# Two transformer blocks in fp32: the last layer norm with a split last bank, a root on ScalarE and a quarter scaled by GpSimd

## The chip, the cores and the metric

The kernel runs on one core of a Trainium2 chip. The metric is device time in microseconds (us), of one launch from start to end. The engines are TensorE (PE, matmuls; PEld is its weight loading), VectorE (DVE), ScalarE (ACT), GpSimd (POOL) and SyncE (SP, which issues the large transfers here). Each runs its own list of instructions in order, and they wait for one another by semaphores.

## The reference, cut to what matters

Two blocks follow each other on 256 tokens of 1024 features, all in fp32. The second block has two layers; each layer ends with a feed-forward part and a layer norm, and the last of these norms is what the change touches:

```python
ALPHA = (2.0 * DEPTH_2) ** 0.25

def layer_norm(x, g, b):
    mu = jnp.mean(x, axis=-1, keepdims=True)
    var = jnp.mean(jnp.square(x - mu), axis=-1, keepdims=True)
    return (x - mu) * lax.rsqrt(var + LN_EPS) * g + b

for l in range(DEPTH_2):                      # 2 layers
    ...                                       # feed-forward, norm, attention, norm
    x = layer_norm(ALPHA * x + 0.5 * swiglu(x, ffn2_w_in[l], ffn2_w_out[l]), ln_g[l, 2], ln_b[l, 2])
```

## The kernel before, in words

The 256 tokens are two tiles (t = 0, 1) of 128, one token to a partition, in `xres[:, t, :]` with 1024 columns. Weights come from HBM in units of 128x2048. Each unit is split by ACT into a high part (`whi`, line 519) and by DVE into the rest (`wlo`, line 527); a product of fp32 precision is three matmuls on them: `tile_mm`, lines 1561 to 1563, 512 columns wide. Line 1924 and line 1929 are the matmuls of the feed-forward's first half, the latter 256 columns wide.

The feed-forward's second half sums into four PSUM banks of 512 columns, bank 4 + 2t + h for token tile t and half h (`down_tile`). In the last step of it, `ffn_pe` goes through the token tiles one after the other: for tile 0 the four column blocks of the last but one unit, then half 0 and half 1 of the last unit, then the same for tile 1. Each half of the last unit is six matmuls, after which PE raises `y_done` (or `used` for the last one), and DVE may add that bank.

`norm_dve` then does, for each tile: two adds of a PSUM bank to `xres` with a sum over the columns (line 1302), the negative mean (line 1307), `cent = (xres + nmean) * ln_g` (line 1312) and, when the root is there, two scalings `xres = cent * lrs + ln_b` of 512 columns (line 1319). Tile 1's adds stand behind tile 0's scalings in DVE's list. `norm_act` (line 856) squares and sums 1024 columns on ACT as soon as the mean is there. `norm_pool` waits for that sum and makes 1 / sqrt(var + eps) on POOL in two instructions, a multiply-add (line 551) and a power of −0.5 (line 553), with a drain between them; the drain makes the first one's result readable for the second. SP waits for each scaling and stores its half tile to the output, four stores of 256 KB (line 485), and waits for all to land.

The function of an ACT instruction may need another table than the loaded one; a load then shows as ACT_TABLE_LOAD. `ffn_act` runs a dummy Silu on one column ahead of its first real one (line 882), so that the load happens there.

Order is set by hand: each engine's list is written out, nothing is planned by a cost model.

Of the kernel before, what the change touches and what calls it, by code (L numbers as in the profile page):

```python
# [8 lines left out]
P = 128  # L9
TOK = 256  # L10
TT = TOK // P
DM = 1024
KD = DM // P
# [9 lines left out]
LAYERS = 2  # L23
# [71 lines left out]
AHEAD = 6  # L95
ATT_ROPES = {0: (P_DQ, 0), 2: (P_DQ, 1), 4: (P_DK, 0), 6: (P_DK, 1)}
# [61 lines left out]
def build(nc, x, positions, ln1_g, w_in, q_norm_a, k_norm_a, q_norm_b, k_norm_b, sinks, w_branch_a,  # L158
# [19 lines left out]
    with ctx:  # L178
# [88 lines left out]
        nmean = little("nmean", [P, TT])  # L267
        mv = little("mv", [P, TT, 2])
# [91 lines left out]
        stored = sem("stored")  # L360
        up_tile = sem("up_tile")
# [78 lines left out]
        def _(sp):  # L440
# [40 lines left out]
            for t in range(TT):  # L481
                for h in range(2):
                    cols = slice(h * BW, (h + 1) * BW)
                    sp.wait_ge(xt_src, 4 * (XT1 + 4 * LAYERS) + 2 * t + h + 1)
                    sp.dma_start(out_r[:, t, cols], xres[:, t, cols]).then_inc(stored, 16)
            sp.wait_ge(stored, 32 * TT)
# [79 lines left out]
        def _(pool):  # L566
# [4 lines left out]
            pool.memset(half[:, :], -0.5)  # L571
            pool.memset(one_lam[:, :, :], 1.0)
# [35 lines left out]
            for l in range(LAYERS):  # L608
                q = 3 * l
                norm_pool(pool, q)  # L610

                for j in range(HALF):
                    pool.wait_ge(o_act, UNITS * l + HALF + j + 1)
                    rsqrt(pool, drs[:, j:j + 1], dss[:, j:j + 1], 1.0 / (2 * HD), EPS2, drs_ready)
                norm_pool(pool, q + 1)
                norm_pool(pool, q + 2)
# [241 lines left out]

        def hidden_act(act, g, u, ffn):

            w = FFN_H if ffn else BW
            for t in range(TT):
                act.wait_ge(used, u + 1)
                act.activation(hid_a[:, t, 0:w], ps[:, t, 0:w], ACT.Silu if ffn else ACT.Relu).then_inc(hid_act, 1)
# [38 lines left out]
        def _(act):  # L903
# [83 lines left out]
            for l in range(LAYERS):  # L987
# [49 lines left out]
                ffn_act(act, u + L_FFN2, g + FFN_S, 2 * l + 1, () if last else (u + L_UNITS, u + L_UNITS + 1))  # L1037
                for t in range(TT):
                    norm_act(act, 3 * l + 2, t)
                    if not last:  # L1040
                        xt_act(act, n + 4, toks=(t,))
# [249 lines left out]
        def norm_dve(dve, q, n, y, u, ffn, last=False):  # L1291
# [39 lines left out]
            if not last:  # L1331
                xt_dve(dve, n, toks=(0,), banks=banks, halves=(0,))
            centre(1)
            if not last:
                xt_dve(dve, n, toks=(0,), banks=banks, halves=(1,))
            scale(1)
            if not last:
                xt_dve(dve, n, toks=(1,), banks=banks)
# [48 lines left out]
        def _(dve):  # L1387
# [118 lines left out]
            for l in range(LAYERS):  # L1506
# [46 lines left out]
                norm_dve(dve, q + 2, n + 4, y + 5, u + L_UNITS - 1, True, last)  # L1553
# [407 lines left out]

        def ffn_pe(pe, u, g, f, n, late=None, banks=XT_BANKS):
# [11 lines left out]
            for t in range(TT):  # L1974
                for k in range(2):
                    for h in range(2):
                        m = down_tile(pe, before, k, h, t, False, False, k, 1 - par)
                if t == 0:
                    pe.wait_ge(lo_done, end + 1)
                    pe.wait_ge(ht_lo_done, 2 * (g + e) + 2)  # L1980
                else:
                    m.then_inc(used, 1)
                for h in range(2):
                    for k in range(2):
                        if t == h == k == 1 and late is not None:
                            late()
                        m = down_tile(pe, end, k, h, t, False, k == 1, k, par)
                    m.then_inc(used if t == h == 1 else y_done, 1)
# [172 lines left out]
```

## Time and profile before

| what | value |
| --- | --- |
| median of 3 runs | 1321.42 us |
| the three runs | 1321.1, 1321.42, 1323.9 us |
| span of the profiled execution, first to last instruction | 1321.2 us |
| PE busy | 1306.3 us, 99% of the span |
| PEld busy | 1102.8 us, 83% |
| DVE busy | 925.2 us, 70% |
| ACT busy | 640.9 us, 49% |
| POOL busy | 70.0 us, 5% |
| granted TensorE clock, mean | 0.997 of full speed |

The profile was taken in an execution of its own, of which it gives the span; the median of the runs is 0.2 us above it. Busy time is the time in which an engine ran an instruction that counts as work. Starts in the timeline are us from the span's start.

### The profile page before, as it was taken

The page shows a single profiled execution, that of the slowest core. Times are in us where ns is not written, and L with a number is a line of the kernel's source. Part 1 is how long each engine was busy: PE and PEld are TensorE (multiplying, and loading weights), DVE is VectorE, ACT ScalarE, POOL GpSimd, SP SyncE. Part 2 cuts the span into 40 slices and gives each one's busy share as a digit, 9 for nine tenths or more (in the row PEclk, how much of TensorE's full clock was granted, in tenths as well). Part 3 has the DMA queues.
Part 4 walks back from the last instruction along what each step waited for, and adds up shares of the span by engine and source line. Part 5 has one row for each costly group of instructions (what it writes and reads, how often), then busy time and mean ns, then how long its engine had stood idle before and what let it go on. Part 6 is the DMA issues. An engine that isn't in the chain of part 4 may idle for free.

```text
span 1321.2 us, 17217 instructions
## 1 busy us (share of the span) xinstructions
PE 1306.3 (99%) x6973; PEld 1102.8 (83%) x6973; DVE 925.2 (70%) x1188; ACT 640.9 (49%) x839; POOL 70.0 (5%) x145
## 2 busy tenths in 40 slices
PE   8999999999999999999999999999999999999997
PEld 7887788888888888887888888888888877888886
DVE  6698777766656666788876666776666888676665
ACT  6777635443335444457554444444443566544441
POOL 4121000000000000000300000000000003000000
PEclk9999999999999999999999999999999999999999
DMA  8543565555555555653565555465555444655550
GB/s 303 192 159 87 138 238 166 190 193 190 194 208 199 191 191 191 191 145 100 171 223 191 192 191 190 154 236 193 187 193 186 160 128 127 231 190 192 188 188 33
DMA packets 155167, 238.11 MB, mean 180 GB/s; under 512 B 4248, under 2 KB 110768, under 8 KB 155088
## 3 DMA queue, kind: packets, MB, share of 16 engines
q1 hardware_dynamic: 154704, 236.47, 54.7%
q8 instruction: 55, 0.90, 0.3%
q0 software_dynamic: 384, 0.54, 0.2%
q14 instruction: 24, 0.20, 0.0%
HBM read 235.95 MB, written 1.05 MB: 179 GB/s over the span
## 4 chain that ended last, share of the span: by engine, by line
issue 86%; PE 10%; POOL 2%; POOLq 1%; ACT 1%; DMA 0%; DVE 0%; SPq 0%; DVEq 0%; ACTq 0%
PE ps L1561 2%; PE ps L1563 2%; PE ps L1562 2%; POOLq L552 1%; POOL drs L553 1%; PE ps L1705 1%; PE ps L1628 1%; POOL lrs L553 1%; PE ps L1714 0%; DMA raw<-in_w_in_dram 0%; PE ps L1729 0%; ACT ebuf L734 0%; PE ps L1683 0%; PE ps L1603 0%; PE ps L1604 0%
## 5 line engine op out<-in xcount | busy, mean ns | idle before, releaser
L527 DVE TENSOR_TENSOR wlo<-raw,whi 128x2048 fp32r<-128x2048 f32 x172 | 391.8, 2287 | 129.2 <-ACT whi L519 129.2
L519 ACT ACTIVATE whi<-raw 128x2048 fp32r<-128x2048 f32 x197 | 369.8, 1905 | 22.3 <-DMA raw<-in_w_up_dram 11.1
L1924 PE MATMUL ps<-xt_both,whi 128*128 128x512 f32 x1504 | 358.7, 390 | 0.0
L1924 PEld LDWEIGHTS ps<-xt_both,whi 128*128 128x128 f32 x1504 | 279.1, 188 | 55.9
L1929 PEld LDWEIGHTS ps<-xt_both,wlo 128*128 128x128 f32 x1504 | 193.4, 191 | 7.6
L1241 DVE TENSOR_REDUCE hid_a<-ps 128x512 f32<-128x1024 f32 (+1 forms) x98 | 115.3, 1177 | 119.5 <-PE ps L1929 119.3
L1929 PE MATMUL ps<-xt_both,wlo 128*128 128x256 f32 x1504 | 195.7, 283 | 0.0
L1561 PE MATMUL ps<-whi,ht_hi 128*128 128x512 f32 x480 | 187.7, 391 | 0.0
L1562 PE MATMUL ps<-wlo,ht_hi 128*128 128x512 f32 x480 | 187.3, 390 | 0.0
L1563 PE MATMUL ps<-whi,ht_lo 128*128 128x512 f32 x480 | 186.8, 389 | 0.0
L877 ACT ACTIVATE hid_b<-hid_a 128x512 f32<-128x512 f32 x40 | 25.2, 631 | 236.5 <-DVE hid_a L1241 236.5
L1561 PE MATMUL ps<-whi,xt_both 128*128 128x512 f32 (+1 forms) x288 | 112.8, 392 | 0.0
L1562 PE MATMUL ps<-wlo,xt_both 128*128 128x512 f32 (+1 forms) x288 | 109.0, 378 | 0.0
L1563 PE MATMUL ps<-whi,xt_both 128*128 128x512 f32 (+1 forms) x288 | 109.0, 378 | 0.0
L1563 PEld LDWEIGHTS ps<-whi,ht_lo 128*128 128x128 f32 x480 | 90.1, 188 | 19.1
L1561 PEld LDWEIGHTS ps<-whi,ht_hi 128*128 128x128 f32 x480 | 90.3, 188 | 17.4
L1562 PEld LDWEIGHTS ps<-wlo,ht_hi 128*128 128x128 f32 x480 | 90.3, 188 | 16.8
L892 ACT ACTIVATE ht_hi<-hid_b 128x512 fp32r<-128x512 f32 x36 | 22.8, 633 | 94.1 <-DVE hid_b L1264 94.1
L500 DVE SCALAR_TENSOR_TENSOR wlo<-raw,g_cols,whi 128x512 fp32r<-128x512 f32 x80 | 56.1, 767 | 13.9 <-ACT whi L493 13.9
L1561 PEld LDWEIGHTS ps<-whi,xt_both 128*128 128x128 f32 x288 | 54.2, 188 | 12.0 <-issue 2.7
L1563 PEld LDWEIGHTS ps<-whi,xt_both 128*128 128x128 f32 x288 | 54.2, 188 | 10.4
L1562 PEld LDWEIGHTS ps<-wlo,xt_both 128*128 128x128 f32 x288 | 54.3, 189 | 8.6
(233 smaller groups left out, 1340.6 us busy)
## 6 DMA issues: line engine op xcount, KB each, us to landing
raw<-in_ffn_w_in_dram SPq DMA_DIRECT2D x80, 1024.0 KB
raw<-in_ffn_w_out_dram SPq DMA_DIRECT2D x44, 1024.0 KB
raw<-in_w_in_dram SPq DMA_DIRECT2D x36, 1024.0 KB
raw<-in_w_up_dram SPq DMA_DIRECT2D x16, 1024.0 KB
raw<-in_w_down_dram SPq DMA_DIRECT2D x16, 1024.0 KB
raw<-in_w_out_dram SPq DMA_DIRECT2D x8, 1024.0 KB
raw<-in_ffn_w_in_dram SPq DMA_DIRECT2D x16, 512.0 KB
raw<-in_w_out_dram SPq DMA_DIRECT2D x8, 512.0 KB
```

The costliest lines, as they stand in the source:

```text
L500: m = dve.scalar_tensor_tensor(wlo[j][:, cols], raw[j][:, cols], g_cols[:, k:k + 1], whi[j][:, cols].bitcast(F32), ALU.mult, ALU.subtract)
L519: act.activation(whi[j][:, :], raw[j][:, :], ACT.Copy).then_inc(hi_done, 1)
L527: dve.tensor_tensor(wlo[j][:, :], raw[j][:, :], whi[j][:, :].bitcast(F32), ALU.subtract).then_inc(lo_done, 1)
L553: pool.tensor_tensor(dst, dst, half[:, 0:dst.shape[-1]], ALU.pow).then_inc(done, 1)
L877: act.activation(hid_b[:, 0, :], hid_a[:, 0, :], ACT.Silu).then_inc(hid_act, 2)
L892: act.activation(ht_hi[s % 2][:, 0:2, :], hidden2, ACT.Copy).then_inc(ht_hi_done, 2)
L1241: return dve.tensor_reduce(hid_a[:, j, k * TOK:(k + n) * TOK].rearrange("p (k n) -> p k n", k=n), ps[:, b:b + n, :].rearrange("p k (j n) - ...
L1561: pe.matmul(o, hi[:, k, tok], block_of(whi, u, b, width), start=start, stop=False)
L1562: pe.matmul(o, hi[:, k, tok], block_of(wlo, u, b, width), start=False, stop=False)
L1563: return pe.matmul(o, lo[:, k, tok], block_of(whi, u, b, width), start=False, stop=stop)
L1924: pe.matmul(o(k).rearrange("p (j n) -> p j n", j=2), whi[w][:, block(b, k)], xt_both[:, :, b, :], start=b == 0, stop=False)
L1929: m = pe.matmul(o(k)[:, 0:TOK], wlo[w][:, block(b, k)], xt_hi[:, b, :], start=False, stop=b == KD - 1)
```

## The change

It touches the last norm of the second layer alone; the other norms stay as they are, and `norm_pool` is no longer called for the last one.

- The last bank of tile 1 is made in two halves by a new function, `last_columns`: first six matmuls of 256 columns into the first half of bank 7, then six into the first half of bank 0, which is free by then. The second half of bank 7 keeps the sum of the earlier units without the last one. DVE adds bank 6, the first half of bank 7, its second half, and then bank 0's 256 columns onto the same columns of `xres`. The sums of the pieces go to four columns of `quarter`, two of which are added in between.
- The mean is written twice, as `nmean` / 32 for ACT and as `nmean` for DVE. ACT squares `xres / 32 + nmean / 32`, so that its sum is the variance itself, drains, and takes the square root with the epsilon as bias; DVE takes the reciprocal of that and drains. A dummy root on one column stands in ACT's list behind the last feed-forward's copies.
- The scaling of tile 1 is cut: DVE does columns 0 to 511 and 512 to 767, POOL does 768 to 1023 in two instructions (a multiplication and an addition, with a drain between them).
- SP stores five pieces: two halves of tile 0, the first half of tile 1, POOL's quarter, DVE's last quarter, in this order.

```diff
+LAST_PIECES = ((0, slice(0, BW)), (0, slice(BW, DM)), (1, slice(0, BW)), (1, slice(DM - BW // 2, DM)),
+               (1, slice(BW, DM - BW // 2)))
+POOL_PIECE = 3
...
-            for t in range(TT):
-                for h in range(2):
-                    cols = slice(h * BW, (h + 1) * BW)
-                    sp.wait_ge(xt_src, 4 * (XT1 + 4 * LAYERS) + 2 * t + h + 1)
-                    sp.dma_start(out_r[:, t, cols], xres[:, t, cols]).then_inc(stored, 16)
-            sp.wait_ge(stored, 32 * TT)
+            for i, (t, cols) in enumerate(LAST_PIECES):
+                sp.wait_ge(pool_rows_out if i == POOL_PIECE else rows_out, 1 if i == POOL_PIECE else min(i + 1, len(LAST_PIECES) - 1))
+                sp.dma_start(out_r[:, t, cols], xres[:, t, cols]).then_inc(stored, 16)
+            sp.wait_ge(stored, 16 * len(LAST_PIECES))
...
+            pool.memset(eps2[:, :], EPS2 / ALPHA ** 2)
...
-                norm_pool(pool, q + 2)
+                if l < LAYERS - 1:
+                    norm_pool(pool, q + 2)
+            t, cols = LAST_PIECES[POOL_PIECE]
+            pool.wait_ge(last_factor, 1)
+            pool.tensor_scalar(cent[:, t, cols], cent[:, t, cols], lrs[:, t:t + 1], None, ALU.mult)
+            pool.drain()
+            pool.tensor_tensor(xres[:, t, cols], cent[:, t, cols], ln_b[:, cols], ALU.add).then_inc(pool_rows_out, 1)
...
+        def last_norm_act(act, q, t):
+
+            act.wait_ge(mean_ready, 2 * q + t + 1)
+            act.activation(squares[:, t, :], xres[:, t, :], ACT.Square, bias=nmean_root[:, t:t + 1], scale=1.0 / ROOT_DM,
+                           accum_out=mv[:, t, 1:2])
+            act.drain()
+            act.activation(lrs[:, t:t + 1], mv[:, t, 1:2], ACT.Sqrt, bias=eps2[:, 0:1]).then_inc(var_ready, 1)
...
+                if last:
+                    act.activation(scratch[:, :], ident[:, 0:1], ACT.Sqrt)
...
+        def last_norm_dve(dve, q, y, u):
...
+            def add(t, a, z, src, total, *ready):
+                xs = xres[:, t, a:z]
+                dve.wait_ge(*ready)
+                dve.scalar_tensor_tensor(xs, src, 0.5 / ALPHA, xs, ALU.mult, ALU.add, accum_out=total)
+
+            def mean(t, first, second):
+                dve.drain()
+                dve.tensor_scalar(nmean_root[:, t:t + 1], first, second, -1.0 / (DM * ROOT_DM),
+                                  ALU.add, ALU.mult).then_inc(mean_ready, 1)
+                dve.tensor_scalar(nmean[:, t:t + 1], first, second, -1.0 / DM, ALU.add, ALU.mult)
+                dve.drain()
...
+            def factor(t):
+                dve.wait_ge(var_ready, 2 * q + t + 1)
+                m = dve.reciprocal(lrs[:, t:t + 1], lrs[:, t:t + 1])
+                dve.drain()
+                return m
...
+            add(0, 0, BW, ps[:, 4, :], sums[:, 0, 0:1], y_done, y + 1)
+            add(0, BW, DM, ps[:, 5, :], sums[:, 0, 1:2], y_done, y + 2)
+            mean(0, sums[:, 0, 0:1], sums[:, 0, 1:2])
+            dve.wait_ge(g_loaded, 16 + 32 * (q + 1))
+            centre(0)
+            factor(0)
+            for t, cols in LAST_PIECES[:2]:
+                scale(t, cols)
+            add(1, 0, BW, ps[:, 6, :], quarter[:, 0:1], y_done, y + 3)
+            add(1, BW, DM - BW // 2, ps[:, 7, 0:BW // 2], quarter[:, 1:2], y_done, y + 4)
+            add(1, DM - BW // 2, DM, ps[:, 7, BW // 2:BW], quarter[:, 3:4], y_done, y + 4)
+            dve.drain()
+            dve.tensor_tensor(quarter[:, 2:3], quarter[:, 0:1], quarter[:, 1:2], ALU.add)
+            add(1, DM - BW // 2, DM, ps[:, 0, 0:BW // 2], quarter[:, 3:4], used, u + 1)
+            mean(1, quarter[:, 2:3], quarter[:, 3:4])
+            centre(1)
+            dve.drain()
+            factor(1).then_inc(last_factor, 1)
+            for i, (t, cols) in enumerate(LAST_PIECES[2:]):
+                if 2 + i != POOL_PIECE:
+                    scale(t, cols)
...
+        def last_columns(pe, u, par):
+
+            tok = slice(P, TOK)
+            for q, o in enumerate((ps[:, 7, 0:BW // 2], ps[:, 0, 0:BW // 2])):
+                for k in range(2):
+                    a = (2 * k + 1) * BW + q * BW // 2
+                    hi, lo = (w[SLOT_OF[u]][:, a:a + BW // 2] for w in (whi, wlo))
+                    pe.matmul(o, ht_hi[par][:, k, tok], hi, start=q == 1 and k == 0, stop=False)
+                    pe.matmul(o, ht_hi[par][:, k, tok], lo, start=False, stop=False)
+                    m = pe.matmul(o, ht_lo[par][:, k, tok], hi, start=False, stop=k == 1)
+                m.then_inc(y_done if q == 0 else used, 1)
```

## Rows read from the trace of the kernel before

**Rows 1.** The page: span, and busy time of PE and PEld.

```profile
span 1321.2 us, 17217 instructions
PE 1306.3 (99%) x6973; PEld 1102.8 (83%) x6973; DVE 925.2 (70%) x1188; ACT 640.9 (49%) x839; POOL 70.0 (5%) x145
```

**Rows 2.** Stretches: busy us (count) of PE, PEld, DVE, ACT, POOL, clock, DMA.

```profile
1314.00:1321.20 7.20, 0.00 (x1) 0.00 (x0) 3.72 (x8) 1.24 (x2) 0.74 (x2) 0.67 0.37 137
```

**Rows 3.** Timeline, tile 0's root and PE's last bank: start, duration, engine, line.

```profile
1309.63 1.15 ACT L856 ACTIVATE squares<-xres,nmean 128x1024 f32<-128x1024 f32 x1 [4.83 <-DVE nmean L1307]
...
1310.68 0.19 ACT L856 ACTIVATION_READ_ACCUMULATOR squares<-xres,nmean 128x1 f32 x1
...
1312.17 1.41 DVE L1319 SCALAR_TENSOR_TENSOR xres<-cent,lrs,ln_b 128x512 f32<-128x512 f32 x2 [1.20 <-POOL lrs L553]
...
1312.48 0.39 PE L1561 MATMUL ps<-whi,ht_hi 128*128 128x512 f32 x1
...
1313.61 0.39 PE L1563 MATMUL ps<-whi,ht_lo 128*128 128x512 f32 x1
```

**Rows 4.** Timeline, tile 1 from its adds to its scalings.

```profile
1313.51 0.68 DVE L1302 SCALAR_TENSOR_TENSOR xres<-ps,xres 128x512 f32<-128x512 f32 x1
...
1314.12 0.68 DVE L1302 SCALAR_TENSOR_TENSOR xres<-ps,xres 128x512 f32<-128x512 f32 x1
...
1314.89 0.21 DVE L1307 TENSOR_SCALAR nmean<-sums 128x1 f32<-128x1 f32 x1
...
1315.20 1.28 DVE L1312 SCALAR_TENSOR_TENSOR cent<-xres,nmean,ln_g 128x1024 f32<-128x1024 f32 x1
1316.19 0.19 ACT L856 ACTIVATION_READ_ACCUMULATOR squares<-xres,nmean 128x1 f32 x1
1316.46 0.19 POOL L551 TENSOR_SCALAR lrs<-mv 128x1 f32<-128x1 f32 x1 [4.32 <-ACT squares L856]
1316.80 0.54 POOL L553 TENSOR_TENSOR lrs<-lrs,half 128x1 f32<-128x1 f32 x1
1317.38 1.41 DVE L1319 SCALAR_TENSOR_TENSOR xres<-cent,lrs,ln_b 128x512 f32<-128x512 f32 x2 [0.89 <-POOL lrs L553]
```

**Rows 5.** Timeline of SP at the last store; DMA issues with us to landing.

```profile
1318.82 0.33 SPq L485 DMA_DIRECT2D out_dram<-xres  x1
...
out_dram<-xres SPq DMA_DIRECT2D x4, 256.0 KB, 2.0
```

**Rows 6.** Groups by form, whole span: busy us, mean ns, idle before.

```profile
L606 POOL TENSOR_SCALAR gates<-gates 128x1024 f32<-128x1024 f32 x4 | 5.0, 1240 | 44.0 <-ACT gates L686 44.0
L553 POOL TENSOR_TENSOR rstd<-rstd,half 128x10 f32<-128x10 f32 x2 | 4.5, 2254 | 0.3
...
L739 ACT ACTIVATE esink<-sink,ntop 128x1 f32<-128x1 f32 x16 | 3.8, 286 | 0.0
...
L1097 DVE TENSOR_TENSOR ob_lo<-ps,ob_hi 128x256 fp32r<-128x256 f32 x4 | 1.7, 420 | 1.5 <-ACT ob_hi L754 1.5
...
L1080 DVE RECIPROCAL rden<-den 128x1 f32<-128x1 f32 x8 | 1.2, 154 | 0.3 <-ACT ebuf L729 0.3
```

**Rows 7.** Timeline of PEld: eight weight loads for 256 columns, then the next.

```profile
1298.96 1.13 PEld L1929 LDWEIGHTS ps<-xt_both,wlo 128*128 128x128 f32 x8
...
1300.02 1.70 PEld L1924 LDWEIGHTS ps<-xt_both,whi 128*128 128x128 f32 x8
```

**Rows 8.** Timeline, DVE (first of a pair, then the pair) and POOL at once.

```profile
110.83 0.74 DVE L500 SCALAR_TENSOR_TENSOR wlo<-raw,g_cols,whi 128x512 fp32r<-128x512 f32 x1
110.83 2.20 DVE L500 SCALAR_TENSOR_TENSOR wlo<-raw,g_cols,whi 128x512 fp32r<-128x512 f32 x2
111.34 1.15 POOL L606 TENSOR_SCALAR gates<-gates 128x1024 f32<-128x1024 f32 x1 [7.60 <-ACT gates L686]
```

**Rows 9.** Groups by form, whole span: table loads at line 882, squares at 856.

```profile
L856 ACT ACTIVATE squares<-xres,nmean 128x1024 f32<-128x1024 f32 x12 | 13.8, 1153 | 29.8 <-DVE nmean L1307 29.8
...
L882 ACT ACT_TABLE_LOAD x3 | 3.8, 1283 | 0.1
```

More of the change, by code:

```diff
@@ L12 @@
 DM = 1024
+ROOT_DM = 32
+assert ROOT_DM ** 2 == DM
 KD = DM // P
@@ L267, in build @@
         nmean = little("nmean", [P, TT])
+        nmean_root = little("nmean_root", [P, TT])
+        quarter = little("quarter", [P, 4])
+        eps2 = little("eps2", [P, 1])
         mv = little("mv", [P, TT, 2])
@@ L360, in build @@
         stored = sem("stored")
+        rows_out = sem("rows_out")
+        last_factor = sem("last_factor")
+        pool_rows_out = sem("pool_rows_out")
         up_tile = sem("up_tile")
@@ L1037, in _ @@
                 ffn_act(act, u + L_FFN2, g + FFN_S, 2 * l + 1, () if last else (u + L_UNITS, u + L_UNITS + 1))
+                if last:
+                    act.activation(scratch[:, :], ident[:, 0:1], ACT.Sqrt)
                 for t in range(TT):
-                    norm_act(act, 3 * l + 2, t)
-                    if not last:
+                    if last:
+                        last_norm_act(act, 3 * l + 2, t)
+                    else:
+                        norm_act(act, 3 * l + 2, t)
                         xt_act(act, n + 4, toks=(t,))
@@ L1289, in ffn_dve, with norm_dve @@
                 split_lo_half(dve, v, 1)
-        def norm_dve(dve, q, n, y, u, ffn, last=False):
+        def norm_dve(dve, q, n, y, u, ffn):
             def add(t, h):
@@ L1330, in norm_dve @@
             mean(1)
-            if not last:
-                xt_dve(dve, n, toks=(0,), banks=banks, halves=(0,))
+            xt_dve(dve, n, toks=(0,), banks=banks, halves=(0,))
             centre(1)
-            if not last:
-                xt_dve(dve, n, toks=(0,), banks=banks, halves=(1,))
+            xt_dve(dve, n, toks=(0,), banks=banks, halves=(1,))
             scale(1)
-            if not last:
-                xt_dve(dve, n, toks=(1,), banks=banks)
+            xt_dve(dve, n, toks=(1,), banks=banks)
@@ new lines, in last_norm_dve, with centre, scale @@
+        def last_norm_dve(dve, q, y, u):
[9 more added lines that the diff above has]
+                dve.drain()
+            def centre(t):
+                dve.scalar_tensor_tensor(cent[:, t, :], xres[:, t, :], nmean[:, t:t + 1], ln_g[:, :], ALU.add, ALU.mult)
+            def factor(t):
[3 more added lines that the diff above has]
+                return m
+            def scale(t, cols):
+                dve.scalar_tensor_tensor(xres[:, t, cols], cent[:, t, cols], lrs[:, t:t + 1], ln_b[:, cols],
+                                         ALU.mult, ALU.add).then_inc(rows_out, 1)
+            add(0, 0, BW, ps[:, 4, :], sums[:, 0, 0:1], y_done, y + 1)
[19 more added lines that the diff above has]
+                    scale(t, cols)
@@ L1552, in _ @@
                 ffn_dve(dve, u + L_FFN2, g + FFN_S, () if last else (u + L_UNITS, u + L_UNITS + 1))
-                norm_dve(dve, q + 2, n + 4, y + 5, u + L_UNITS - 1, True, last)
+                if last:
+                    last_norm_dve(dve, q + 2, y + 5, u + L_UNITS - 1)
+                else:
+                    norm_dve(dve, q + 2, n + 4, y + 5, u + L_UNITS - 1, True)
         def block_of(w, u, b, width=BW):
@@ L1983, in ffn_pe @@
                 for h in range(2):
+                    if t == h == 1 and late is None:
+                        last_columns(pe, end, par)
+                        break
                     for k in range(2):
-                        if t == h == k == 1 and late is not None:
+                        if t == h == k == 1:
                             late()
```

## Prediction

> **What bounds the kernel now.** I read the page first: TensorE (PE) is busy for 99% of the span, so nearly all of the 1321.2 us belongs to matmuls, which this change leaves alone except for the last bank [rows 1]. Then the stretches: after 1314.0 PE has nothing to do, and the 7.2 us up to the end of the span hold 3.7 us of VectorE (DVE), 1.2 us of ScalarE (ACT) and 0.7 us of GpSimd (POOL) [rows 2]. This tail is a chain in which one engine waits for another, and it is all that the change can move, apart from what happens to its start. Last I read the timeline of the tail, instruction by instruction, because the chain of waits merges it too much.
>
> In the tail the reader is to see five links. (1) PE ends its last matmul at 1313.61 + 0.39 = 1314.00 [rows 3]. (2) DVE adds the last two banks of token tile 1, at 1313.51 and 1314.12; the second follows the first by 0.61 us and starts 0.12 after PE's end, so here DVE and PE end almost together. The mean follows at 1314.89, which is 0.77 after the start of the last add. (3) ACT's sum of squares ends at 1316.19 + 0.19 = 1316.38. (4) POOL computes the root in two instructions from 1316.46 on, and DVE starts to scale at 1317.38, so the root costs 1.00 us from ACT's end. (5) Two scalings take 1.41, to 1318.79 [rows 4]; SP issues the last of four stores 0.03 later, which takes 0.33 to issue and lands 2.0 after [rows 5]; the span ends 2.4 after the issue's start. For token tile 0 the same root takes 1.30 (1310.87 to 1312.17) [rows 3], and DVE goes straight from its scalings to the adds of tile 1 (1312.17 to 1313.51, 1.34 us): a quicker root there lets the adds of tile 1 start sooner.
>
> The profile's page gives a span of 1321.2; the three runs have a median of 1321.42, so 0.2 lies around the span. I sum changes against the span and add 0.2.
>
> **The change, part by part.** *The root on ACT.* It removes two POOL instructions per token tile, and adds a drain, a root of 128x1 on ACT, and a reciprocal and a drain on DVE. A root is not in the trace; the nearest row is another function of ACT on 128x1 with a bias column, 0.286 [rows 6]. I take that; from below, no cost at all would make the step 0.29 cheaper, and the dearest nearby bound is a whole squaring of 1024 columns, 1.15 [rows 3], which nothing in a 128x1 form suggests. The reciprocal is 0.154 [rows 6]. Between engines I take the 0.08 of the row from ACT to POOL (1316.38 to 1316.46) for each drain, and 0.04 from POOL's end (1316.80 + 0.54 = 1317.34) to DVE's start for a wait on DVE [rows 4]. From ACT's end to the scalings: 0.08 + 0.286 + 0.04 + 0.154 + 0.08 = 0.64 us, against 1.30 for tile 0 and 1.00 for tile 1. Saved: 0.66 and 0.36. The bounds of the sum are 0.35 and 1.5.
>
> The table for the root is loaded ahead: a load lasts 1.283 [rows 9] and stands after ACT's last copy, behind which ACT idles 4.83 us before the squaring [rows 3]. It costs nothing; without this cover it would cost its 1.28. The removed norm of POOL frees nothing else, since nothing is queued behind it. One more small memset at the start of POOL is hidden by its wait for the first weights.
>
> *A second nmean.* Each mean now writes two columns, the scaled one first, which releases ACT as before. The centring starts later by at most one small DVE instruction (0.15). It ended at 1315.20 + 1.28 = 1316.48 [rows 4], and becomes about 1316.70 (with the late start of the mean, below), while the root comes at 1316.82: hidden, by 0.1. If that cover were gone, at most 0.15.
>
> *The last bank on PE.* Six matmuls of 512 columns, 0.226 apart (1312.48 to 1313.61 in five steps) [rows 3], become twelve of 256. Weight loads of a 256-column group are (1300.02 − 1298.96) / 8 = 0.133 apart [rows 7]. Twelve take 1.59 against 1.36, so PE ends 0.22 later, 1314.22 (the last starts at 1312.48 + 11 x 0.133 = 1313.94 and takes 0.28). The first half of the bank is there at 1312.48 + 5 x 0.133 + 0.28 = 1313.43.
>
> *The adds of tile 1.* The scalings of tile 0 start at 1310.87 + 0.64 = 1311.51, so the first add starts 1.34 later, at 1312.85 (its bank is ready at 1312.48 − 0.23 + 0.39 = 1312.64). At +0.61, 1313.46, come two adds of 256 columns. A DVE instruction from PSUM of 256 columns takes 0.42 [rows 6] against 0.68, so each is 0.27 shorter: the second starts at 1313.80, and from there to the next small instruction it is 0.77 − 0.27 = 0.50: 1314.30. That one sums two columns, at most 0.15: 1314.45. By then PE is done (1314.22), so the split bank is not what DVE waits for. The last add and its drain take 0.50 again, and the mean starts at 1314.95, **0.06 later than before** (1314.89). Three small adds with one more sum eat up what tile 0 saved. Bounds: −0.1 with small instructions that overlap, +0.2 without. So the gain of the bank's split is nil: 0.66 earlier at the start, 0.06 later at the end.
>
> *The scalings.* Tile 1's can start at 1316.38 + 0.06 + 0.64 = 1317.08, 0.30 earlier. DVE now has 512 and 256 columns; the latter is 0.27 shorter than 0.74, 0.47, and alone it would end at 1317.08 + 0.67 + 0.47 = 1318.22. POOL has 256 columns in two instructions, a multiplication and an addition. The multiplication: 193 ns at 1 column [rows 4] and 1240 at 1024 [rows 6] make 1.02 ns a column, so 0.19 + 0.26 = 0.45. An addition of two tensors on POOL is not in the trace. Bounds: 0.45 if the second input is free; 0.54 (a power of 128x1 [rows 4]) + 256 x 2.05 = 1.07 if each input costs a pass. A power on POOL costs far more per column: 2.254 at 10 columns [rows 6] against 0.54 at one, 0.19 a column, which would make 49 us of 256. I leave that end out of the range with a small chance of its own, because the multiplication by the same engine shows that plain arithmetic costs 1.02 ns a column, and an addition is nearer to it. I take 0.7, between the other two. The GPSIMD Engine Reference of the Trainium skill (Elementwise, side-by-side cycle accounting) gives about 2.6 cycles per column for such an addition, 0.56 us at its 1.2 GHz before any overhead; my sum would be the same within 0.1 by it.
>
> Do POOL and DVE run side by side? The trace has this case. DVE's pair of 128x512 with both inputs in SBUF normally takes 1.41 [rows 4]. At 110.83 such a pair took 2.20; its first had the usual 0.74, and POOL's multiplication ran from 111.34 to 112.49. The second ended at 113.03, 0.54 after POOL [rows 8]: it stood still while POOL read, and ran afterwards. So the two take turns. The last scalings read cent and ln_b, both in SBUF, so this applies to them. If DVE is first: it lets go at 1317.08 + 0.67 = 1317.75; POOL multiplies to 1318.20; DVE's quarter ends 0.54 − 0.27 = 0.27 later, 1318.47; POOL adds to 1319.17. SP's queue holds the stores in the order half, POOL's quarter, DVE's last quarter, so the last store waits behind POOL's: issues at 1319.20 and 1319.53, against 1318.82 before, **+0.7**. If POOL is first (1317.08 to 1317.53), DVE's half ends 0.54 later at 1318.07, POOL adds to 1318.77, the issues stand at 1318.80 and 1319.13: **+0.3**. The last instructions before are a near tie (a wait on POOL against a drain on DVE, 0.08 each), so I take +0.5.
>
> *The stores.* One more issue (0.33) is in the sums. The last store has 128 KB instead of 256. Landing is 2.0 for 256 KB [rows 5]; smaller may be quicker by anything from 0 to half of it. I take 0.2.
>
> Sum: +0.5 − 0.2 = +0.3; 1321.2 + 0.3 + 0.2 around = **1321.7 us**. It is no change that can be measured: about 0.2% (2.6 us) is what a measurement of this kernel tells from none.
>
> **Rivals.**
> 1. *POOL and DVE do not hinder each other.* POOL: 1317.08 + 0.45 + 0.15 + 0.7 = 1318.38; issues at 1318.41 and 1318.74, so −0.1, and −0.3 with the smaller store: **1321.1**. For it: the multiplication is short and might fit into DVE's gaps. Against it: rows 8.
> 2. *A table switch comes onto the path (slower).* If the set with the root lacks the square, ACT must load before each root. The loads before the squares hide in ACT's idle time (4.83, and as much for tile 1); those before the two roots do not: tile 0's delays its scalings by 1.28 and with them the adds, tile 1's adds 1.28 again: 2 x 1.283 = 2.57, **1324.3**. It decides as slower once the two cost over 2.4. Against it: the square of this norm ran twelve times with no load at its line, while the loads at the line that prepares Silu stand elsewhere [rows 9]; it seems to be in every set that was in use. The Trainium skill, in ScalarE: Activation LUTs (What ACT_TABLE_LOAD costs), puts 1.38 us of drain on top of each switch; by that the rival would give 1327.0. No run here shows such a drain. The preload would take 2.7 of its 4.83 and still be hidden.
> 3. *The whole saving shows* (DVE's adds start without small gaps, POOL's add is 0.45, the store is twice as quick): 0.3 + 0.4 + 0.3 gives **1320.4**. A gain over 0.2% would need more than a third of the whole tail, and none of its parts is that large.
>
> **How the numbers follow.** Forecast (turns taken, 1321.4 to 1322.1) 0.60; rival 1 0.25; rival 3 0.06; rival 2 0.05; anything else, a POOL addition many times dearer above all, 0.04. The range 1320.4 to 1323.0 leaves out rival 2 and the last, and on its upper side holds what the three runs differ by. Faster by over 0.2% 0.02, within 0.2% 0.92, slower 0.06.
>
> **What would show it.** Right: the root and reciprocal put DVE's scalings of tile 0 at about 1311.5 and those of tile 1 near 1317.1; the mean of tile 1 stands near 1314.9; one of DVE's or POOL's last instructions is stretched well beyond 0.75 or 0.45; the last store is issued at 1319.1 to 1319.5, behind POOL's. Wrong: a table load between a square and a root; an addition on POOL above 1.1; a last issue before 1318.8; PE's end beyond 1314.5; or PE's stretches before 1307 not the same as now, which no part of the sum foresees.

## The result, and the profile after

The changed kernel is slower: 1325.56 us median (1325.0 to 1327.39, 5 runs) against 1321.42. The ratio to the kernel before is 1.0029, 95% interval 1.0018 to 1.0040. The forecast was 1321.7, no change that can be measured; the range ended at 1323.0. The profiled execution took 1326.12 with a span of 1324.0. The executions of the kernel before fall into two groups, at 1320.8 to 1322.6 and at 1322.9 to 1325.8 us, so a median of few can jump by 2 us, and the interval of the ratio is what counts.

The tail first. Rows of the timeline of the changed kernel, which answer to [rows 3, 4] (start, duration, engine, line):

```profile
1312.28 0.18 ACT L880 ACTIVATION_READ_ACCUMULATOR squares<-xres,nmean_root 128x1 f32 x1
...
1312.81 0.29 ACT L883 ACTIVATE lrs<-mv,eps 128x1 f32<-128x1 f32 x1 [0.34 <-issue]
...
1313.38 1.41 DVE L1392 SCALAR_TENSOR_TENSOR xres<-cent,lrs,ln_b 128x512 f32<-128x512 f32 x2
...
1314.71 0.68 DVE L1373 SCALAR_TENSOR_TENSOR xres<-ps,xres 128x512 f32<-128x512 f32 x1
...
1315.39 0.28 PE L2051 MATMUL ps<-whi,ht_lo 128*128 128x256 f32 x1
...
1316.75 0.21 DVE L1377 TENSOR_SCALAR nmean_root<-quarter 128x1 f32<-128x1 f32 x1
...
1318.06 0.19 ACT L880 ACTIVATION_READ_ACCUMULATOR squares<-xres,nmean_root 128x1 f32 x1
...
1318.90 1.29 DVE L1392 SCALAR_TENSOR_TENSOR xres<-cent,lrs,ln_b 128x512 f32<-128x512 f32 x2
1318.91 1.47 POOL L632 TENSOR_SCALAR cent<-cent,lrs 128x256 f32<-128x256 f32 x1 [183.49 <-DVE lrs L1387]
1320.53 0.72 POOL L634 TENSOR_TENSOR xres<-cent,ln_b 128x256 f32<-128x256 f32 x1
```

And SP's timeline at the last store of the changed kernel:

```profile
1321.65 0.43 SPq L496 DMA_DIRECT2D out_dram<-xres  x1
```

The same matmuls start 1.6 us later here than in the kernel before (matmul number 6951 at 1310.22 against 1308.63), so 1.6 has to be taken off. Then the scalings of tile 1 start at 1317.3, 0.1 earlier than before, but GpSimd's multiplication lasts 1.47, and its quarter is done at 1320.53 + 0.72 = 1321.25. The last store, behind it in SP's queue, is issued at 1321.65, which is 1320.05 in the time of before, 1.2 later. The tail, from a matmul that all kernels have (number 6951) to the end of the span, grew from 12.62 to 13.74 us: **1.1 us lost in the tail**.

A smaller part lies outside the span. The time exceeds the span by 1.74 to 1.87 us in every execution on record of a kernel with four stores, and by 2.07 to 2.24 in every one of a kernel with five: 0.3 us, in the changed kernel too. Whether the fifth store is the reason, or something else that those kernels share, was not tried.

That is not all. Two rows of the stretches of the kernel before, then of the changed kernel (us; busy us with count of PE, PEld, DVE, ACT, POOL; clock; DMA share; GB/s):

```profile
20.00:24.00 4.00, 4.00 (x18) 3.00 (x17) 4.00 (x7) 4.00 (x8) 2.95 (x26) 1.00 0.67 159
...
32.00:36.00 4.00, 4.00 (x19) 3.34 (x18) 3.87 (x6) 2.01 (x4) 2.01 (x3) 1.00 0.48 139
```

```profile
20.00:24.00 4.00, 4.00 (x18) 3.03 (x17) 4.00 (x7) 4.00 (x8) 2.16 (x22) 1.00 0.78 54
...
32.00:36.00 4.00, 1.53 (x7) 1.01 (x6) 4.00 (x7) 4.00 (x8) 4.00 (x8) 1.00 0.70 222
```

In the changed kernel TensorE stands still for 2.5 of the four microseconds from 32. From 20 to 24 the DMA engines are busier than before and move a third as much. The waits of the changed kernel in its first 45 us (who waited for whom, us in total, times, longest; "issue" is a wait for nothing that the profile shows) lead back:

```profile
POOL lrs L562 <- issue: 5.6, 1, 5.6
...
ACT proj L671 <- POOL lrs L564: 4.9, 1, 4.9
...
DVE pos_f L1421 <- DMA dlam<-in_diff_lambda_dram: 3.0, 1, 3.0
...
PE ps L1641 <- ACT proj L671: 2.5, 1, 2.5
```

TensorE waits for ACT's first projection reads, these for the norm on GpSimd, and GpSimd stands 5.6 us behind its constants' loads, until `dlam` has landed: the profile names no releaser there, but GpSimd goes on at 27.76, 0.5 after the landing (issued at 18.72, landed 8.5 later), and in the kernel with the dummy root below at 26.52, 0.6 after it (18.14 + 7.8). The rows of DMA issues say how long the loads took, first of the kernel before, then of the changed kernel (KB, us to landing):

```profile
dlam<-in_diff_lambda_dram POOLq DMA_DIRECT2D x1, 256.0 KB, 3.9
...
sink<-in_swa_sink_dram POOLq DMA_DIRECT2D x1, 8.0 KB, 4.0
```

```profile
dlam<-in_diff_lambda_dram POOLq DMA_DIRECT2D x1, 256.0 KB, 8.5
...
sink<-in_swa_sink_dram POOLq DMA_DIRECT2D x1, 8.0 KB, 6.5
```

The change touched none of these loads, and in the code near them only one memset; three new small tiles also move where they land by 96 bytes. Among the packets of GpSimd's queue, those of 256 and 512 bytes (16 each, the two `sink` loads) took 18 and 32 ns on average in the kernel before, and 878 and 1117 ns in the changed one. The 4 and 64 byte packets of the same queue took 12 and 25 ns in both, so it is these two loads that are slow and not small packets as such. **This loss at the start is the larger part**, and the experiments had to find its cause.

### The profile page after: what moved, and what is told of

Its sections match the earlier page's. It is cut to its first block, busy times and chain, and to the rows that moved or that the text cites. A ratio compares the mean times of both kernels' runs of the same rounds, so it can differ in the third digit from the quotient of the medians.

```text
span 1324.0 us, 17245 instructions
## 1 busy us (share of the span) xinstructions
PE 1305.9 (99%) x6979; PEld 1102.7 (83%) x6979; DVE 926.5 (70%) x1197; ACT 643.1 (49%) x843; POOL 69.8 (5%) x144
## 4 chain that ended last, share of the span: by engine, by line
issue 86%; PE 8%; POOL 2%; ACT 1%; POOLq 1%; DMA 1%; SPq 0%
PE ps L1641 2%; PE ps L1643 2%; PE ps L1642 2%; POOLq L563 1%; POOL drs L564 1%; PE ps L1785 1%; POOL lrs L564 1%; DMA raw<-in_w_in_dram 1%; ACT whi L504 0%; PE ps L1794 0%; PE ps L1809 0%; ACT ebuf L752 0%; PE ps L1763 0%; ACT proj L671 0%; POOL gain L590 0%
```

## The experiments

A table of what each run showed; the text on each follows. Tail: from matmul 6951 to the end of the span. Packets: mean ns of the 256 and 512 byte packets on GpSimd's queue. Stall: by how much TensorE's matmuls slip between number 131 and 141 (near 34 us) against the second profile of the kernel before. Half clock: whether the trace has a stretch of 3.4 us at half the granted clock near 10 us. In the two kernels that load the sinks late, the packets are those of 37 to 40 us.

```
kernel                   median    ratio (95%)               tail   packets     dlam  stall  half clock
before                   1321.42   -                         12.62    18   32   3.9   0.0    yes
before_again             1321.40   one run                   12.63    18   28   4.5   -      no
after                    1325.56   1.0029 (1.0018-1.0040)    13.74   878 1117   8.5   2.7    no
after_again              1325.72   one run                   13.74   905 1020   7.7   1.9    no
after_new_tiles_last     1325.42   1.0025 (1.0017-1.0034)    13.75   766 1096   7.3   1.5    no
before_padded_96         1322.25   0.9999 (0.9989-1.0008)    12.62    18   32   3.9   0.0    no
before_one_memset        1322.47   0.9998 (0.9989-1.0007)    12.55    18   27   4.9   0.0    no
after_memset_late        1325.28   1.0022 (1.0013-1.0030)    13.75  1193  901   5.8   0.0    yes
after_dve_scales_all     1324.64   1.0013 (1.0004-1.0022)    12.73  1003 1036   8.0   2.2    no
before_root_on_act       1323.04   1.0009 (1.0000-1.0017)    12.19   668 1428   8.0   2.1    no
before_dummy_sqrt        1323.72   1.0017 (1.0008-1.0026)    12.62   627 1143   7.8   1.9    no
before_dummy_exp         1324.25   one run                   12.62    18   47   3.9   0.0    yes
after_silu_for_sqrt      1322.94   1.0008 (1.0000-1.0017)    13.46    19   27   4.3   0.0    no
after_gpsimd_alone       1326.11   one run                   14.57  1153  893   6.0   0.0    yes
before_dummy_gelu        1323.91   1.0010 (1.0001-1.0019)    12.61   855 1097   7.5   1.6    no
before_sinks_late        1323.42   1.0004 (0.9995-1.0013)    12.61   109   30   5.3   0.0    no
root_on_act_sinks_late   1323.37   1.0001 (0.9992-1.0010)    12.21   158  686   4.8   0.0    yes
```

The medians of the kernel before in the four sets of runs were 1321.97, 1322.34, 1321.55 and 1321.26; a ratio is made within its set. Where the clock was halved, TensorE was already late by 1.6 to 3.0 us at number 131, and the late norm held it up no more. A stall of 0.0 in such a trace is no proof of a quick start; there the packets and `dlam` tell.

**Addresses.** The three new small tiles stand in the middle of the small ones and move `dlam`, `subg` and the sinks by 96 bytes. One kernel puts them last, one moves the tiles in the kernel before:

```diff
@@ after_new_tiles_last
-        nmean_root = little("nmean_root", [P, TT])
-        quarter = little("quarter", [P, 4])
-        eps2 = little("eps2", [P, 1])
...
         drs = little("drs", [P, TT * 4])
+        nmean_root = little("nmean_root", [P, TT])
+        quarter = little("quarter", [P, 4])
+        eps2 = little("eps2", [P, 1])
@@ before_padded_96
         nmean = little("nmean", [P, TT])
+        pads = [little(f"pad{j}", [P, 1]) for j in range(3)]
```

> The changed kernel, with its three new small tiles (nmean_root, quarter, eps2) allocated behind all the others, so that every older tile has the address it had before the change. Theory A (addresses): moving the small tiles by 96 bytes made the constants' loads from GpSimd's queue slow (dlam lands after 8.5 us instead of 3.9), which holds GpSimd's first norm and costs TensorE 2.7 us near 34 us of the span. Then this kernel has its dlam landing near 4 us, no stall of TensorE at 34 us, and only the tail's cost is left: 1.2 us over the kernel before, about 1322.6. Theory B (timing or chance: the constants' loads collided with the weights' loads in the profiled execution because TensorE's and ScalarE's start was earlier there): no difference to the changed kernel, 1325.5. Theory C (more instructions or semaphores at the start): 1325.5 as well.

> The kernel before, with three unused tiles of one column (96 bytes in all) allocated behind nmean, which moves the later small tiles by as much as the change does; nothing else differs and no instruction is added. Theory A (addresses): 2.7 to 2.9 us slower than before, about 1324.3, with dlam landing at 6 to 9 us and a stall of TensorE near 34 us. Theories B and C: the time of before, 1321.4.

> The kernel before, profiled once more. It shows whether the slow start belongs to an execution or to a kernel. Theory A: TensorE's matmul number 131 at the time of the first profile (33.8 us, or a little earlier without the stretch at half clock that the first profile had), dlam landing at 3.9 us. Theory B: a start like the changed kernel's may appear here too, with dlam at 8 us.

> The changed kernel, profiled once more. Theory A: dlam lands at 6 to 9 us again and TensorE stalls by about 2.7 us near 34 us again. Theory B: the landing may be at 4 us and the stall gone. The tail is as in its first profile in both: GpSimd's multiplication about 1.4 us long, the last store issued 17.2 us after the first matmul of the last but one unit.

Theory A was mine and falls twice: with the old addresses the start stays slow, with the moved ones it stays quick. B falls too: the slow packets came back in each profile of the changed kernel and in none of the kernel before. The second profile of before also mends a number of the prediction: its span is 1319.6 with a time of 1321.40. So 1.8 us lie around a span (2.1 in the changed kernel), and the first profile, with its halved clock, was of an execution 1.6 us slower than this one.

**The memset, and parts of the change.**

```diff
@@ before_one_memset
             pool.memset(half[:, :], -0.5)
+            pool.memset(spare[:, :], 1e-5)
@@ after_memset_late
             pool.memset(half[:, :], -0.5)
-            pool.memset(eps2[:, :], EPS2 / ALPHA ** 2)
...
+            pool.memset(eps2[:, :], EPS2 / ALPHA ** 2)
             pool.drain().then_inc(mask_pool, 1)
@@ after_dve_scales_all
-            pool.tensor_scalar(cent[:, t, cols], cent[:, t, cols], lrs[:, t:t + 1], None, ALU.mult)
-            pool.drain()
-            pool.tensor_tensor(xres[:, t, cols], cent[:, t, cols], ln_b[:, cols], ALU.add).then_inc(pool_rows_out, 1)
...
-                if 2 + i != POOL_PIECE:
-                    scale(t, cols)
+                scale(t, cols)
@@ before_root_on_act (last norm only)
+            act.activation(squares[:, t, :], xres[:, t, :], ACT.Square, bias=nmean_root[:, t:t + 1], scale=1.0 / ROOT_DM,
+                           accum_out=mv[:, t, 1:2])
+            act.drain()
+            act.activation(lrs[:, t:t + 1], mv[:, t, 1:2], ACT.Sqrt, bias=eps2[:, 0:1]).then_inc(var_ready, 1)
...
+                    dve.reciprocal(lrs[:, t:t + 1], lrs[:, t:t + 1])
```

> The kernel before, with one more memset of one column on GpSimd (of an unused tile behind all others) at the place where the changed kernel sets its epsilon, ahead of the constants' loads; nothing else. Theory D (the added memset, or what it moves on GpSimd, makes the constants' loads slow): dlam lands after 7 to 8.5 us instead of 3.9 to 4.5, the packets of 256 bytes on GpSimd's queue take near 1 us instead of 18 ns, and the kernel is 2.7 us slower than before, 1324.5. Theory E (some other part of the change, such as the second table set, the longer lists of instructions or their place in HBM): as before, 1321.7, dlam at 4 us.

> The changed kernel with its epsilon memset moved behind the masks on GpSimd, so that nothing stands ahead of the constants' loads that was not there before. Theory D: dlam lands near 4 us, TensorE's stall near 34 us is gone, and what is left is the tail's 1.2 us: 1322.9. Theory E: 1325.5 and dlam at 7 to 8.5 us.

> The changed kernel with DVE scaling GpSimd's quarter too (three pieces: 512, 256, 256 columns, in the order of the stores), GpSimd idle at the end; the early memset stays. Theory of the lock (GpSimd's multiplication took 1.47 us instead of 0.45 because DVE's two scalings went first and let it in only behind both): the last store is issued about 1.2 us earlier relative to TensorE's last matmul than in the changed kernel, and the time is 1.2 us less, 1324.4, if the slow start stays (Theory E does not care about this part, unless the instructions of GpSimd's quarter are what makes the start slow; then 1321.6). Rival (GpSimd's instruction is slow by itself on this shape, no lock): the same gain in this kernel, so the two are told apart not here but in a kernel in which GpSimd works while DVE rests.

> The kernel before with the root alone moved to ACT and the reciprocal to DVE (one table preload, a second nmean column, the epsilon set behind the masks); the last bank is whole and DVE scales all in two halves as before. My sum: 0.66 us less for tile 0, whose adds then wait for TensorE's last bank (ready at 0.12 before the add now); 0.36 less for tile 1, and with the adds sooner by 0.1, a tail 0.3 to 0.45 shorter than before. Theory E, if the second table set or the changed lists slow the start: plus 2.7, so 1324.2; if it is the parts that are absent here, 1321.4 (before 1321.8).

The memset is not it (Theory D falls). The tail comes apart cleanly: the root on ACT alone makes it 12.62 to 12.19, **0.43 shorter**, as summed (0.3 to 0.45), though in part by luck: the scalings of tile 0 came 0.39 earlier, not 0.66. It cost little, because the last add would have waited for TensorE's last bank in any case, as it does in that kernel:

```profile
1314.43 0.69 DVE L1319 SCALAR_TENSOR_TENSOR xres<-ps,xres 128x512 f32<-128x512 f32 x1 [0.23 <-PE ps L1590]
```

With the split bank, three scalings in place of two and the fifth store added, but DVE scaling all, it is 12.73, so these together cost **0.54**. Of it 0.35 stands at tile 1's mean already and belongs to the split bank's adds; the third scaling and the store make the rest. GpSimd's quarter brings 13.74, **1.01 more**. And the root alone already has the slow start.

**The table set.** What the kernels with the slow start shared was Sqrt, a function that nothing else in the program uses, with an ACT_TABLE_LOAD of its own (1.28 us at 1306.4 in the changed kernel).

```diff
@@ before_dummy_sqrt (before_dummy_exp: ACT.Exp; before_dummy_gelu: ACT.Gelu)
                 ffn_act(act, u + L_FFN2, g + FFN_S, 2 * l + 1, () if last else (u + L_UNITS, u + L_UNITS + 1))
+                if last:
+                    act.activation(scratch[:, :], ident[:, 0:1], ACT.Sqrt)
@@ after_silu_for_sqrt
-                    act.activation(scratch[:, :], ident[:, 0:1], ACT.Sqrt)
+                    act.activation(scratch[:, :], ident[:, 0:1], ACT.Silu)
...
-            act.activation(lrs[:, t:t + 1], mv[:, t, 1:2], ACT.Sqrt, bias=eps2[:, 0:1]).then_inc(var_ready, 1)
+            act.activation(lrs[:, t:t + 1], mv[:, t, 1:2], ACT.Silu, bias=eps2[:, 0:1]).then_inc(var_ready, 1)
@@ after_gpsimd_alone
             factor(1).then_inc(last_factor, 1)
+            dve.wait_ge(pool_rows_out, 1)
```

> The kernel before with one thing added: the dummy square root of one column on ACT behind the last feed-forward, with the table load that it needs. Its result is not used. So far the start was slow (packets of 256 bytes on GpSimd's queue near 1 us instead of 18 ns, dlam landing after 6 to 8 us) in all five profiles of kernels that use Sqrt, and in none of the four that do not. Theory F (one more set of tables in the program, from wherever it sits): slow start, GpSimd's packets near 1 us, and 2 us more, 1323.8, although the added instruction runs 1300 us later and is hidden. Theory G (another thing that those five kernels share: fewer norms on GpSimd, the reciprocal, the second nmean): as before, 1321.8.

> The same as the dummy square root, but with Exp, whose table set the kernel uses anyway: one more table load and one more ACT instruction, no new set. Theory F: packets of 18 ns and dlam at 4 to 5 us, as before. Rival F2 (any further table load or ACT instruction does it): slow packets here too.

> The changed kernel with Silu in place of both uses of Sqrt, so that the factor of the last norm is not the reference's; all instructions stay in number, order and size but the table load. Theory F: fast start, dlam at 4 to 5 us, and only the tail's cost of 1.1 us over the kernel before stays: 1322.9, TensorE's end as in the kernel before plus 0.1 to 0.2. Theory G: 1325.4 and slow packets.

> The changed kernel with DVE waiting for GpSimd's quarter before it scales its own two pieces of tile 1, so that GpSimd runs alone. Theory of the lock: GpSimd's multiplication of 128x256 takes about 0.45 us (0.3 to 0.5) instead of 1.47, its addition 0.6 to 0.7. Rival (the form itself is slow, with its factor read from a column): 1.4 us here too. The tail is longer in both, by the 1.3 us or more that DVE rests, less what GpSimd gains.

> The kernel before with a dummy of one column of Gelu, in place of the square root of the earlier dummy: a third set, used nowhere else. Theory F (any further set of tables in the program makes the two sink loads at the start slow): packets of 256 and 512 bytes near 1 us, dlam at 7 to 8 us, 1323.8 like the dummy root. Rival F3 (only the set of Sqrt, by its size or place): packets of 18 ns, dlam at 4 us, 1321.7.

One dummy root at 1300 us, whose result nobody reads, slows the loads at 20 us: its waits in the first 45 us are those of the changed kernel again.

```profile
POOL lrs L551 <- issue: 4.9, 1, 4.9
...
ACT proj L653 <- POOL lrs L553: 4.0, 1, 4.0
...
PEld ps L1563 <- ACT proj L653: 2.0, 1, 2.0
```

The kernel is 1.0017 (1.0008 to 1.0026) of before, 2.2 us. With Gelu in place of the root the packets and `dlam` are slow in the same way, and the ratio is 1.0010 (1.0001 to 1.0019); Exp, whose set the kernel has anyway, leaves the packets quick (its single time, 1324.25, lies among the runs of before, 1320.75 to 1324.26, and its clock was halved, so the time tells nothing). And the changed kernel with Silu for Sqrt, its instructions else the same, has quick packets and 1322.94 instead of 1325.3 to 1325.6. Its tail is 0.28 shorter as well, because ACT's last instruction for tile 0 did not start late. The rivals G, F2 and F3 fall. Theory F agrees with all of it, but one rival is left: Sqrt and Gelu are new functions as well as functions of further sets. A new function out of a set in use was not tried, so "the set" is the likelier reading and not a shown one.

GpSimd alone, in the timeline of that kernel:

```profile
1318.08 0.94 POOL L632 TENSOR_SCALAR cent<-cent,lrs 128x256 f32<-128x256 f32 x1 [183.49 <-DVE lrs L1387]
1319.16 0.72 POOL L634 TENSOR_TENSOR xres<-cent,ln_b 128x256 f32<-128x256 f32 x1
1319.92 1.15 DVE L1392 SCALAR_TENSOR_TENSOR xres<-cent,lrs,ln_b 128x512 f32<-128x512 f32 x2 [1.94 <-POOL xres L634]
```

The multiplication takes 0.94 alone, not 0.45 and not 1.47. Both halves of the question were right in part: the form is slow by itself (0.5 above my estimate), and DVE beside it costs 0.53 more; DVE's pair, 1.15 alone, took 1.29 beside GpSimd, 0.14 more.

**A way round.** If the sinks' packets are what blocks the queue, loading them later should free the start.

```diff
-            pool.dma_start(sink1[:, :], sinks[0, :].partition_broadcast(P)).then_inc(const_loaded, 16)
-            pool.dma_start(sink2[:, :, :], swa_sink_2.partition_broadcast(P)).then_inc(const_loaded, 16)
...
             pool.drain().then_inc(mask_pool, 1)
+            pool.dma_start(sink1[:, :], sinks[0, :].partition_broadcast(P)).then_inc(sinks_loaded, 16)
+            pool.dma_start(sink2[:, :, :], swa_sink_2.partition_broadcast(P)).then_inc(sinks_loaded, 16)
```

> The kernel before with the loads of the two sinks (the 32 and 64 bytes per partition whose packets are the slow ones) moved on GpSimd's queue from the constants to behind the masks, near 35 us, with a semaphore of their own. A control: in the kernel before their packets take 18 and 32 ns, so moving them gives at most the 1.1 us of issue that they take on GpSimd ahead of its first norm, and TensorE waits for that norm by little or nothing: 1321.3 to 1321.8.

> The kernel before with the root on ACT and both sinks loaded late. If the slow start goes through those two loads (they block the ring in front of subg and dlam, GpSimd's drain waits for dlam, its norm and with it ACT's first projection reads come late), then TensorE's start is as in the kernel before, and only the tail's gain of 0.43 us is left: 1321.3, the first version at or below the kernel before. If the slowness is of GpSimd's queue as a whole in a program with this set, then subg and dlam are slow without the sinks, and the time is 1323.0 as with the root alone.

With the sinks late, `dlam` lands after 4.8 us in the kernel that has the root and its set, against 8.0 with the sinks in front of it; subg and dlam are not slow by themselves, and the tail keeps its gain (12.21). The sinks' own packets are still slow at 39 us (158 and 686 ns, against 109 and 30 in the control), where nothing waits for them. In the kernel before the move is worth nothing, as forecast (1.0004, 0.9995 to 1.0013).

The time of the way round was forecast as 1321.3, and its median is 1323.37, but six of its ten executions of usual length lie in the upper group that the kernel before has as well. The ratio is 1.0001 (0.9992 to 1.0010), and its interval overlaps that of the root's kernel (1.0000 to 1.0017). Four of the ten lie at 1320.75 to 1322.08, below all eleven of the root's kernel (1322.33 and up), which speaks for a start that is quick again. A gain over the kernel before is not shown. One of its eleven executions took 3366 us, which I can't explain. No version here beats the kernel before.

## Why the prediction was wrong, by its steps

- **"The table for the root is loaded ahead ... It costs nothing": the step that failed.** The load itself was hidden, as said (1.28 us at 1306.4, with ACT idle until 1311.2). But using the root costs at the other end of the program: 1.5 to 2.7 us of stall where the clock was not halved, 2.2 us in the dummy's median. The last sign of being wrong that I had named, TensorE's stretches before 1307 not the same as before, is the one that came true. Rival 2 feared the set for a switch between square and root; there was none. The Trainium skill, in ScalarE: Activation LUTs (What ACT_TABLE_LOAD costs), adds 1.38 us of drain to a load; here ACT's next instruction started 0.02 after the load's end (1307.70 behind 1306.40 + 1.28), so no such drain shows.
- **The multiplication on GpSimd, 0.45: mis-sized.** A slope from one wide row and one narrow row gave half of the 0.94 that it takes alone. The one row of [rows 6] had constants as factors, this one reads its factor from a column; whether that is the difference was not tried. The addition, 0.7, was 0.72.
- **Turns with DVE: right in kind, off in size.** I had DVE wait or GpSimd wait for one piece; in fact GpSimd's 1.47 spanned both of DVE's pieces and DVE lost only 0.14. The last store was issued 1.23 later, not 0.3 to 0.7. Rival 1 (no hindrance) is excluded by the 0.53. The SBUF — State Buffer page of the Trainium skill (SBUF: two separate sides) says that a VectorE instruction with two inputs in SBUF and a GpSimd one that reads SBUF exclude each other for whole instructions. The direction agrees, but both were done 1.48 after the first began, not in 0.94 + 1.15 one after the other, so part of the time overlaps.
- **The root, 0.64 from ACT's end: right for tile 1 (0.65), short for tile 0.** There ACT's root started 0.35 after the squares' end, 0.34 of it with nothing that the profile shows to wait for; it took 0.92. The scalings began 0.28 later than I had them, and with them the adds and tile 1's mean: 0.26 after the old time instead of 0.06.
- **The split bank: right that it gains nothing.** PE ended at 1315.67 − 1.60 = 1314.07, not 1314.22; DVE was the later one. The mean of tile 1 came 0.26 after its old time, beyond the +0.2 that I had as a bound, and the split's adds cost 0.35 beside the whole bank with the same root.
- **The memset, the second nmean, the order of the stores: as said.** The memset changed nothing (0.9998). But the order was a poor one: DVE's last quarter was done at 1318.90 + 1.29 = 1320.19 and GpSimd's at 1321.25, so with DVE's quarter stored first the last issue could have stood at 1321.28 instead of 1321.65, by my estimate 0.4 earlier. It was not tried.
- **The smaller store**: 1.9 to landing, against 2.0; I had taken 0.2 off.
- **The sum**: 0.3 forecast. The tail lost 1.12, the time outside the span 0.3 and the start, by the dummy root's median, about 2.2: 3.6 together, inside the interval of the ratio (2.4 to 5.3 us). Also wrong was 0.2 around the span: it is 1.8, and 2.1 in the changed kernel.

What stays open is why the use of Sqrt or Gelu makes just the packets of the two sink loads some thirty to sixty times slower, while the smaller ones of 4 and 64 bytes on the same queue stay at 12 to 15 and 24 to 27 ns in every trace. It may be where the program's data or the tables lie in memory; no run here could set that.

## What to carry to other kernels

A first use of a function from a table set of its own can be a change to the whole program: compare the two traces from the start, not only where the edit is, and try the dummy alone. A quarter of an elementwise step is worth giving to GpSimd only if its two instructions, priced from a row of the same form and with DVE at work beside it, end before DVE would have done it itself: 1.47 + 0.72 here against the 0.4 that DVE takes for 256 more columns, 1.54 for its three pieces against 1.15 for two. Constants that are needed late don't belong in a queue in front of those that a drain waits for; here that took `dlam`'s landing from 8.0 to 4.8 us in the kernel with the root, and gave nothing in the kernel before, whose loads were quick.

## What the runs showed that I had not expected

- A function of one more set of ACT tables (Sqrt or Gelu; once in a dummy at 1300 us is enough) goes with packets of 256 bytes at 0.6 to 1.2 us on GpSimd's DMA queue at 20 us, in nine profiles of nine that load the sinks there; in the six without such a set and with that load they take 18 or 19 ns.
- In 5 of 17 profiles TensorE's granted clock was half (1.2 instead of 2.4 GHz) for 3.4 us near 10 us, in kernels of every kind. TensorE was then 1.6 to 3.0 us late at 34 us (up to 0.9 in the others, ahead of the stall), and in kernels with the slow loads their stall vanished behind it: two delays of which only the longer shows. The times agree: all eleven executions with the dummy root took 1323.2 or more, where the kernel before, in the same set, has 15 of 21 at 1322.4 or less and six at 1323.1 to 1324.3.
- ACT's root came 0.34 to 0.36 us late behind tile 0's squares in all eight traces that have it, and 0.07 behind tile 1's. GpSimd's root in the kernel before had the same pattern, 1.30 us for tile 0 and 1.00 for tile 1 [rows 3, 4]. With Silu in the root's place tile 0's instruction came 0.07 late. So on ACT the delay goes with the first real use of the root after its table's load. GpSimd has it without any such load, so the load is not shown to be the reason, and it stays open.
